# A hybrid encoder trunk on one core: weight splits of the first in-projection moved ahead of gate and recurrence steps

## The reference

```python
def conv_lru_mixer(h, w_in, conv_a_w, conv_b_w, conv_b_b, lru_wa, lru_ba, lru_wx, lru_bx, lru_lambda, w_out):
    z = h @ w_in                      # (512, 1024) @ (1024, 2560)
    a_val, a_gb, a_gc, b_gate, b_in = ...   # five groups of 512 columns
    y_a = a_gb * depthwise_conv(a_gc * a_val, conv_a_w, 1)
    xr = depthwise_conv(b_in, conv_b_w, 1) + conv_b_b
    h_rec = (rglru(xr, ..., False) + rglru(xr, ..., True))   # forward and reversed recurrence
    y_b = jax.nn.gelu(b_gate) * h_rec.astype(h.dtype)
    return jnp.concatenate([y_a, y_b], axis=-1) @ w_out
```

## Time and profile before

| | |
|---|---|
| time of three executions | 1431.94, 1432.92, 1432.91 us; median 1432.91 |
| profiled execution | 1432.89 us, of which the profiled span is 1431.1 us |
| TensorE matmul | 1259.3 us busy, 88% of the span |
| TensorE weight load | 852.2 us, 60% |
| VectorE | 950.7 us, 66% |
| ScalarE | 616.6 us, 43% |
| GpSimd | 167.0 us, 12% |

### The profile page before, as it was taken

The page is one execution under the profiler, slowest core; times in us unless marked ns, Lnnn a source line. Parts: engine busy times, 40 slices in busy tenths (PEclk is TensorE's granted clock), DMA queues, the critical chain, the costliest instruction groups (busy, mean ns, idle before and its releaser), DMA issues.

```text
span 1431.1 us, 14567 instructions
## 1 busy us (share of the span) xinstructions
PE 1259.3 (88%) x4997; PEld 852.2 (60%) x4997; DVE 950.7 (66%) x1331; ACT 616.6 (43%) x792; POOL 167.0 (12%) x177
## 2 busy tenths in 40 slices
PE   2999899949999999983899999999499999999881
PEld 2566665546766666741788854467367666667430
DVE  8678876476777777713866588856667777776114
ACT  3486301235555555402422167734265555554001
POOL 6100000010000000002000047710100000000002
PEclk9999899969999999997899999999599999999996
DMA  9936673258999999883375230023689999998445
GB/s 353 327 114 240 222 288 151 95 198 305 374 364 367 365 382 377 306 313 132 123 287 179 88 118 1 0 74 117 247 308 382 365 377 363 376 370 304 146 181 191
DMA packets 79552, 353.14 MB, mean 247 GB/s; under 512 B 12632, under 2 KB 12816, under 8 KB 70544
## 3 DMA queue, kind: packets, MB, share of 16 engines
q1 hardware_dynamic: 67616, 327.28, 61.8%
q0 software_dynamic: 8352, 20.46, 4.0%
q10 hardware_dynamic: 3536, 4.79, 0.9%
HBM read 334.15 MB, written 28.31 MB: 253 GB/s over the span
## 4 chain that ended last, share of the span: by engine, by line
PE 75%; DVE 13%; DMA 5%; ACT 4%; issue 3%; POOL 1%; SPq 0%; DVEq 0%; ACTq 0%; POOLq 0%
PE ps L1865 24%; PE ps L1876 17%; PE ps L1967 8%; PE ps L1785 4%; PE ps L1856 3%; DVE scratch L1035 3%; PE ps L1792 2%; PE ps L1851 2%; PE ps L1752 2%; PE ps L2011 2%; PE ps L2039 2%; PE ps L2025 2%; PE ps L1870 1%; DMA x_res<-in_x_dram 1%; PE ps L1747 1%
## 5 line engine op out<-in xcount | busy, mean ns | idle before, releaser
L1876 PE MATMUL ps<-slab_ring,scratch 128*128 128x512 f32 x560 | 246.5, 593 | 3.4 <-ACT scratch L943 2.1
L1865 PE MATMUL ps<-slab_ring_r,gate_rows_r 128*128 128x512 f32 x512 | 201.7, 394 | 0.0
L1876 PEld LDWEIGHTS ps<-slab_ring,scratch 128*128 128x128 f32 x560 | 105.8, 190 | 124.2 <-issue 117.3
L1457 DVE TENSOR_TENSOR slab_ring_r<-slab_ring,h_t_r 128x2048 fp32r<-128x2048 f32 x64 | 143.9, 2287 | 16.8 <-ACT h_t_r L862 16.8
L1967 PE MATMUL ps<-slab_ring_r 128*128 128x512 f32 x384 | 121.4, 398 | 2.4 <-DVE h_t_r L1092 2.4
L862 ACT ACTIVATE h_t_r<-slab_ring 128x2048 fp32r<-128x2048 f32 x64 | 118.6, 1901 | 0.0
L1865 PE MATMUL ps<-h_t_r,gate_rows_r 128*128 128x512 f32 x256 | 105.6, 413 | 12.2 <-issue 7.3
L891 ACT ACTIVATE scratch<-ps,mod_ab 128x128 f32<-128x128 f32 x128 | 48.1, 457 | 144.4 <-PE ps L1851 144.4
L1865 PEld LDWEIGHTS ps<-slab_ring_r,gate_rows_r 128*128 128x128 f32 x512 | 97.9, 191 | 19.1 <-issue 0.5
L1865 PE MATMUL ps<-h_t_r,scratch_r 128*128 128x512 f32 x256 | 102.2, 399 | 0.0
L1457 DVE TENSOR_TENSOR slab_ring_r<-slab_ring,x_norm_r 128x2048 fp32r<-128x2048 f32 x32 | 73.3, 2292 | 40.6 <-ACT x_norm_r L862 40.6
(11 more groups left out here) (329 smaller groups left out, 2210.7 us busy)
## 6 DMA issues: line engine op xcount, KB each, us to landing
slab_ring<-in_expert_w_gate_dram SPq DMA_DIRECT2D x35, 2048.0 KB, 10.1
slab_ring<-in_expert_w_up_dram SPq DMA_DIRECT2D x35, 2048.0 KB, 10.2
slab_ring<-in_expert_w_down_dram SPq DMA_DIRECT2D x35, 2048.0 KB, 10.3
mod_ring<-in_mod_w_dram SPq DMA_DIRECT2D x40, 512.0 KB, 4.7
y_rows<-scratch SPq DMA_DIRECT2D x35, 512.0 KB, 10.8
slab_ring<-in_mod_w_dram SPq DMA_DIRECT2D x32, 512.0 KB, 4.8
slab_ring<-in_mod_w_dram SPq DMA_DIRECT2D x12, 1024.0 KB, 11.3
slab_ring<-in_w_qkv_dram SPq DMA_DIRECT2D x6, 2048.0 KB, 12.2
```

The costliest lines, as they stand in the source:

```text
L1457: tt_(rest, w, top.bitcast(F32), ALU.subtract).then_inc(low_ready[c], 1)
L1865: ins = pe.matmul(ps[:, bank, :], x, w, start=(kt == 0 and i == 0), stop=(kt == KT - 1 and i == 2))
L1876: ins = pe.matmul(ps[:, 5 + h, :], hidT[:, f, :], w[:, 2 * f + h, :], start=(f == 0), stop=(f == FT - 1))
```

## The change

Four calls change places. On VectorE both halves of the split of group 2 and the second half of group 3 stand earlier, and on ScalarE the high copy of that second half. The counts of `mod_acc` around them are cut anew. No instruction is added or removed, and no load is moved in SyncE's order.

```diff
@@ ScalarE, inside the loop over j
             take_z(5 + 2 * j)
+            if j == 3:
+                high_in(3, 1)
             for d in range(2):
                 act.wait_ge(mult_ready, 4 * j + d + 1)
                 act.activation(th[d], th[d], ACT.Sqrt, scale=0.25).then_inc(m_ready, 1)
-            if j >= 2:
-                high_in(3, j - 2)
+            if j == 2:
+                high_in(3, 0)
@@ VectorE
         conv_b(3)
-        mod_acc(2, 0, 3)
+        low_in(2, 0)
+        mod_acc(2, 0, 2)
         gates_in(0)
-        mod_acc(2, 3, 3)
+        low_in(2, 1)
+        mod_acc(2, 2, 3)
         gates_out(0)
-        low_in(2, 0)
-        mod_acc(2, 6, 2)
-        low_in(2, 1)
+        mod_acc(2, 5, 3)
         gates_in(1)
@@ VectorE
         gates_in(3)
+        low_in(3, 1)
         mod_acc(4, 3, 2)
         gates_out(3)
-        low_in(3, 1)
         mod_acc(4, 5, 3)
```

## The result

The changed kernel took 1436.94 us in the median of ten executions (1434.05 to 1438.08), beside 1433.2 us for the kernel before (1431.71 to 1434.77). The ratio is 1.0021, with a 95% interval of 1.0013 to 1.0029: 3.0 us slower (1.9 to 4.2). The two medians are 3.7 us apart; the ratio and its interval are what the text goes by. The forecast was 2.9 us slower. The three are +3.0, +1.0 and +3.2 us, 2.4 in the mean, so that the first came within 0.1 us of the forecast is in part luck.

The account below looks back on a forecast made before the run. The prediction took VectorE's fixed list, not TensorE's waits, to set the end of the changed stage. It summed 1432.89 + 1.97 (late scan_done) + 0.94 (wait for ScalarE's copy) = 1435.8 us, range 1433.3 to 1437.8.

Parts of the forecast that it names:

- The bound: Stage end: VectorE's fixed list sets it, busy 29.33 of 30.70 us from 160.4 to 191.1; TensorE starting earlier gives nothing.
- The first term: Steps 0 to 1: split (2, 1) ahead of gates_out(0) delays scan_done, ScalarE's step 1 and group 3's slab, +1.97 us.
- The second term: Step 3: VectorE waits for ScalarE's copy ahead of split (3, 1), +0.94 us, or 0.86 if the copy overlaps.
- first sign of being wrong: Steps 0 to 1: the prediction is wrong if ScalarE's step 1 starts before 100.5; 100.96 was forecast.
- The other two: Wrong if split (3, 1) finds its copy ready, or VectorE's list from 163 to split (4, 1) is under 28 us.
- The sum: Whole kernel: 1432.89 + 1.97 + 0.94 = 1435.8 us, +0.20%; both terms and no more, chance 0.50.
- What was costed at nothing: Split (2, 0) hidden in step 0's idle time; group 4's slab 5.1 us later, covered; ScalarE's later square roots hidden.
- The clock: Ahead of tile 18: a gap of about 2.7 us lets TensorE's clock fall, +1.5 us, 1437.3 in all; chance 0.18.
- The step that failed: Tiles 16 and 17 were to take 12.37 us, as tiles 14 and 15 did, ending at 191.5 ahead of tile 18.
- the order makes no difference: Whole kernel: same instructions, same waits in sum, scan_done not holding ScalarE, 1432.9 us; chance 0.07.
- TensorE's earlier tiles count: If VectorE's list from 160 had room, tile 14's 3.7 us gain reaches the end, 1429.2 us; chance 0.08.
- Worse starving: Slices of vector 5 land too late behind group 4's slab, 1438 us or more; chance 0.03.

Follow-up runs that it names:

- The three: Three comparisons of the same changed kernel against the kernel before, no edit between them: ratios 1.0021, 1.0007 and 1.0022.
- (2, 0) early: Kernel before with split (2, 0) ahead of gates_in(0) and split (2, 1) behind gates_out(0), step 3 as before: ratio 1.0005.
- (4, 1) early: Kernel before with split (4, 1) moved ahead of two slices, val(3) and mod_take(4): ratio 0.9983.
- the early slab: Changed kernel with group 3's slab issued ahead of vector 3's last four slices and the first out-projection slab: ratio 0.9989 on the kernel before.
- the first run of steps 0 and 1: Kernel before with only the moves of both group 2 splits, step 3 as before: ratio 1.0011, and 1.0006 when run again.
- the last: The combination with the slab of group 3 issued early on SyncE: ratio 0.9951 on the kernel before.
- the split (3, 1) behind the slices: Changed kernel with split (3, 1) behind mod_acc(4, 3, 2), still ahead of gates_out(3): ratio 1.0004 on the kernel before.
- step 3 only: Kernel before with only the copy and split (3, 1) moved, steps 0 and 1 as before: ratio 1.0003.
- both splits ahead of the gates: Kernel before with both group 2 splits and two slices ahead of gates_in(0), two slices instead of three ahead of gates_out(0): ratio 0.9981.
- the combination: Kernel before with both group 2 splits ahead of gates_in(0), split (3, 1) behind two slices, and split (4, 1) early: ratio 0.9976.

## Why the prediction was right

**The bound.** The step that the end of the stage is VectorE's list and not TensorE's waits held in the three traces of the changed kernel and in those of each of its two parts. It is narrower than the prediction made it: in the traces of "(2, 0) early" and "(4, 1) early" the chain runs on TensorE from tile 14 to the out-projection. The two stalls that the change removed came back as 6.31 and 7.17 us at the next instruction that waits for VectorE, as the prediction put it ("about 6" and "about 7").

**The first term** was put at 1.97 us. Measured: 1.95 at the end of `gates_in(1)`, 1.96 at the issue of the slab (1.96 or 1.97 in six traces), 1.88 and 2.06 at the split (4, 1) in the runs with this part alone. Its mechanism, `scan_done`, was shown by the pair that differs only in the side of `gates_out(0)` on which the split (2, 1) stands, and its way through the slab by the early slab. The waits ahead of `gates_in(1)` were put at 0.6 and 2.3 and measured 0.58 and 2.46 us.

**The second term** was put at 0.94, with 0.86 as the lower bound if the copy overlaps the end of the tile ahead. It does, 150.11 against 149.64 + 0.58, and the wait is 0.87 us; the shift with this part alone is 0.78. The value to take was the bound.

**The times as they were given.** The prediction gave its signs in the time of the trace of before, and this trace runs 0.64 us ahead of it at the mark (84.08 against 84.72). Its first sign of being wrong, that ScalarE's step 1 starts before 100.5, came true to the letter, at 100.31, and not in substance: lined up at the mark it is 100.95, where 100.96 was forecast. In the same way the slab was issued at 124.10 (forecast 124.1) and the split (4, 1) started at 191.55 (forecast 191.7). A sign of this kind has to be given from a mark. The other two did not come: the wait of 0.87 us was there, and the list took 190.91 - 162.51 = 28.40 us.

**The sum** of 2.91 us is 2.73, 2.60 and 2.63 in the three traces. It is 0.2 to 0.3 too large: 0.07 from the second term, and the rest mostly between the slab's issue (+1.96) and the end of `gates_in(3)`, which is at 152.12 - 0.87 - 84.08 = 67.17 us against 150.03 - 84.72 = 65.31 before, +1.86. The slab landed 14.81 us after its issue instead of the 14.88 that the prediction kept.

**What was costed at nothing.** The split (2, 0) in the idle time of step 0: shown, -0.26 us with that move alone. The slab of group 4, put 5.1 us later: 4.95 (164.70 - 84.08 = 80.62 against 160.39 - 84.72 = 75.67), without effect. The square roots: `gates_out(3)` never waited.

**The clock.** The prediction put the gap ahead of tile 18 at about 2.7 us and the clock's fall there at 0.18. In the three executions of the changed kernel the gap was 1.79, 1.83 and 1.19 us. The step that failed is the 12.37 us for tiles 16 and 17: they took about 13.3 (178.31 to 193.35 - 1.79), since the granted clock behind the 7.17 us of idle time was 0.50 for 3.4 us and low into the next stretch. The low clock narrowed the gap that should have brought the next fall. The fall itself is real, as the first run of steps 0 and 1 shows. But the reading behind it, 2.47 us harmless and 2.78 us costly, does not hold: the last section has gaps of 2.5 and of 2.8 us with either outcome. The chance of 0.18 rested on too few rows.

**The other rivals.** That the order makes no difference, or that TensorE's earlier tiles count, was excluded by the runs. "Worse starving" did not come: the largest wait of VectorE for a slice in the changed kernel was 0.17 us.

## What to carry to other kernels

A step moved into an engine's idle time is only free if it stands on the side of that idle time from which nothing is released to another engine: here 2.2 us ahead of one `scan_done` moved the idle time to the next step and went on through a load queue to the end, while the same instruction on the other side, or further forward, cost nothing or gained. When TensorE waits for an engine whose list is full, removing one of its waits moves it to the next. And where a load is issued behind small ones that wait for buffers, the small ones pace it: the reordering of one queue was worth 3.4 us in the stage, more than any single move of compute here.

## What the runs showed of the hardware

The scatter. In the fourteen profiled executions the code from the out-projection on is the same, and the time from its start to the end of the span is between 1428.1 - 205.16 = 1222.9 us and 1431.0 - 203.41 = 1227.6 us. The start of `gates_in(0)`, behind the same code on TensorE and ScalarE, lies between 84.06 and 85.67 us. So single executions scatter by 4 to 5 us, more than every change studied but the last, and for edits in one stage the marks inside it are worth more than the total.

The clock was a part of it. Of the ten executions of the changed kernel in the first comparison, the four of 1434.05 to 1434.73 us show a mean granted clock of 0.938 or 0.939, the five of 1437.31 us and more one of 0.935 or 0.936 (the one at 1436.58 us shows 0.938). With the same kernel, tile 18 began behind a gap of 2.62 us and lost 1.61 us to the low clock in one execution, and began behind 1.28 us and lost nothing in another. The gaps in a run of 2.46 (the split (3, 1) behind the slices) and 2.08 us (step 3 only) brought no fall at tile 18.

The length of a gap alone does not tell. TensorE's gate products in two more runs (the first row is of "both splits ahead of the gates", the others of the combination; in brackets the gap ahead):

```profile
107.48 5.37 PE L1762 MATMUL ps<-scratch,gate_rows 128*128 128x512 f32 x8 [2.81 <-DVE scratch L1200]
...
107.59 3.67 PE L1764 MATMUL ps<-scratch,gate_rows 128*128 128x512 f32 x8 [2.81 <-DVE scratch L1202]
...
126.39 5.33 PE L1764 MATMUL ps<-scratch,gate_rows 128*128 128x512 f32 x8 [2.51 <-DVE scratch L1202]
```

Behind the same gap of 2.81 us the eight took 5.37 us in one kernel and 3.67 us in the other (granted clock over the first 3.4 us 0.67, and 1.00 over the first 3.5). A gap of 2.51 us was followed by 5.33 us (clock 0.50), where 2.47 us in the kernel before left them at 3.67. The clock also fell without a gap. In the kernel before TensorE ran 16 matmuls of one column each (L1708) from 173.03 on, 3.74 us, and was busy all the while; the stretches with these and behind them:

```profile
173.00:177.30 4.30, 4.30 (x20) 4.22 (x20) 4.23 (x3) 1.91 (x1) 0.00 (x0) 0.99 0.40 159
177.30:180.80 3.50, 3.50 (x10) 2.70 (x9) 3.39 (x4) 0.00 (x0) 0.00 (x0) 0.52 0.68 204
```

The same kind of burst, 16 matmuls of L1708, stands ahead of tile 12, which began behind only 1.01 us of idle time and ran at 0.52 for 5.4 us. So to remove the wait ahead of such a tile need not bring the full clock back.

That the outcome varies fits what the Trainium skill ("TensorE: Matmul & The Clock Gate", Part 1) says of a monitor that runs free of the kernel, with a place that varies from run to run; no run here shows the monitor itself.
